# The last expert's down weights in column quarters, the second half as two transfers of 512 KB

## The reference

```python
def expert_block(args):
    e, xb = args
    gate, up = jnp.split(xb @ w_gate_up[e], 2, axis=-1)
    return (jax.nn.silu(gate) * up) @ w_down[e]
...
y = y_buf[dest] * gate_sorted[:, None].astype(xt.dtype)
out = jnp.zeros((N, D), xt.dtype).at[tok_sorted].add(y)
...
return rms_norm(h, norm_final)
```

## Time and profile before

| what | value |
|---|---|
| median of 3 runs | 660.54 us (660.26 to 660.78) |
| profiled execution | 661.26 us |
| its span, first to last instruction | 659.4 us |
| mean granted TensorE clock | 0.922 |
| TensorE busy | 514.9 us, 78% |
| VectorE, ScalarE busy | 228.5 us, 181.2 us |
| DMA | 238.12 MB, mean 361 GB/s |
| experts' weights in the chain that ended last | 43% |

### The profile page before, as it was taken

How to read it: one execution, slowest core, us unless ns; L and a number is a source line. 1 busy time by engine, 2 the same in 40 slices (tenths; PEclk the granted TensorE clock), 3 DMA queues, 4 the chain that set the end, 5 groups by cost and what they waited for, 6 DMA issues and landing times.

```text
span 659.4 us, 13368 instructions
## 1 busy us (share of the span) xinstructions
PE 514.9 (78%) x5842; PEld 376.5 (57%) x5842; DVE 228.5 (35%) x474; ACT 181.2 (27%) x400; POOL 27.2 (4%) x50
## 2 busy tenths in 40 slices
PE   8999999999999977886665854866585486658663
PEld 7988998789888755554333522533263253325431
DVE  4696896764653532221211311121121112112113
ACT  7659557264442021110111110010111001011113
POOL 1220202200000000000000000000000000000000
PEclk9999999999999998999878977887897788789888
DMA  8944744496579999999999999999999999999992
GB/s 332 372 157 170 313 166 151 135 415 218 192 295 371 373 393 428 425 438 435 436 433 427 427 429 432 432 435 429 435 429 438 438 435 435 429 409 426 426 396 82
DMA packets 16005, 238.12 MB, mean 361 GB/s; under 512 B 1760, under 2 KB 2016, under 8 KB 3424
## 3 DMA queue, kind: packets, MB, share of 16 engines
q1 hardware_dynamic: 15680, 236.94, 86.4%
q10 hardware_dynamic: 288, 0.63, 0.3%
HBM read 236.51 MB, written 1.05 MB: 360 GB/s over the span
## 4 chain that ended last, share of the span: by engine, by line
PE 47%; DMA 44%; DVE 2%; ACT 2%; issue 1%; SPq 1%; another core or an unknown queue 1%; POOL 1%; ACTq 0%; DVEq 0%; POOLq 0%
DMA ring<-in_w_expert 43%; PE psum L626 15%; PE psum L934 9%; PE psum L609 9%; PE psum L965 4%; PE psum L656 2%; PE psum L802 1%; PE psum L779 1%; PE psum L594 1%; SPq L457 1%; DMA res<-in_x 1%; PE psum L865 1%; PE psum L958 1%; POOL stat L1378 1%
## 5 line engine op out<-in xcount | busy, mean ns | idle before, releaser
L934 PE MATMUL psum<-ring,xg 128*32 128x256 f32 x2048 | 157.5, 469 | 85.1 <-DMA ring<-in_w_expert 78.0
L934 PEld LDWEIGHTS psum<-ring,xg 128*32 128x32 f32 x2048 | 75.8, 133 | 155.4 <-DMA ring<-in_w_expert 84.3
L626 PE MATMUL psum<-split_w,split_act 128*128 128x512 f32 x432 | 102.3, 393 | 0.9 <-DVE res L1642 0.9
L626 PEld LDWEIGHTS psum<-split_w,split_act 128*128 128x128 f32 x432 | 80.2, 188 | 17.8 <-DVE res L1642 1.3
L1314 ACT ACTIVATE small<-psum 128x128 f32<-128x128 f32 x32 | 8.9, 277 | 280.5 <-PE psum L934 280.5
L1855 DVE SCALAR_TENSOR_TENSOR small<-small,psum 128x128 f32<-128x128 f32 x32 | 9.2, 288 | 204.7 <-ACT small L1314 204.7
L1467 DVE TENSOR_TENSOR split_w<-landing,split_w 128x2048 fp32r<-128x2048 f32 x29 | 66.2, 2290 | 33.8 <-ACT split_w L1105 33.7
L1105 ACT ACTIVATE split_w<-landing 128x2048 fp32r<-128x2048 f32 (+1 forms) x31 | 57.5, 1863 | 46.5 <-PE psum L609 22.8
L1866 DVE COPY ybuf<-psum 32x128 f32<-32x128 f32 x128 | 37.2, 291 | 77.0 <-PE psum L965 76.2
L609 PE MATMUL psum<-split_act,split_w 128*128 128x256 f32 x480 | 58.2, 283 | 0.0
L609 PEld LDWEIGHTS psum<-split_act,split_w 128*128 128x128 f32 x480 | 57.8, 192 | 0.4 <-issue 0.3
(11 more groups left out here) (191 smaller groups left out, 407.7 us busy)
## 6 DMA issues: line engine op xcount, KB each, us to landing
ring<-in_w_expert SPq DMA_DIRECT2D x20, 6144.0 KB, 47.8
ring<-in_w_expert SPq DMA_DIRECT2D x23, 2048.0 KB, 31.6
landing<-in_dense SPq DMA_DIRECT2D x29, 1024.0 KB, 5.5
ring<-in_w_expert SPq DMA_DIRECT2D x26, 1024.0 KB, 8.3
res<-in_x SPq DMA_DIRECT2D x2, 512.0 KB, 4.2
landing<-in_dense SPq DMA_DIRECT2D x2, 512.0 KB, 7.2
work<-in_mem SPq DMA_DIRECT2D x1, 1024.0 KB, 13.8
ybuf<-in_late SPq DMA_DIRECT2D x1, 512.0 KB, 17.6
```

What stands on the lines that cost most here:

```text
L626: i = mm(b, tokens_of(src[t], k0 + k, h), w[a][:, k, :], start=first and k == 0 and n == 0, stop=last and k == CT - 1 and n == 2)
L934: i = mm(half[SLOTS * strip:SLOTS * strip + SLOTS], xg[:, CT * part + k, SLOTS * j:SLOTS * j + SLOTS], w[:, k, :, P * strip:P * strip + P] ...
```

## The change

`lay_out_experts` orders the down weights by column quarters: the 16 KB of a partition hold four blocks of 4 KB, one for each 256 output columns, and in a block the four chunks of the contraction. `expert_down` and `ov_down_w` follow; strip s of a side is in quarter s // 2 of that side. Whole-expert and whole-unit transfers are as they were.

The second half of the last down unit comes in two transfers of 512 KB, each with its own semaphore (`loaded[u][1]` and the new `last_quarter`). On TensorE, both scatters of columns 0 stand ahead of the products of that half. Each quarter is multiplied by `last_down(q)`, two strips for each chunk, quarter 0 into bank 4 and quarter 1 into bank 6; ScalarE and VectorE copy one strip each; `last_scatter(q)` adds 256 columns to both token halves.

```diff
 def lay_out_experts(inputs):
-    down = ....reshape(EXPERTS, CT, P, 2, 512).transpose(0, 2, 3, 1, 4)
+    down = ....reshape(EXPERTS, CT, P, 2, 2, 256).transpose(0, 2, 3, 4, 1, 5)
...
 def refill_down(g, j, by_sides):
                 sp.wait_ge(y_done, 2 * BATCH * g + (2 * (j - BATCH) + 2))
                 if by_sides:
-                    load_expert(BATCH * g + j, j, 2)
+                    u, w = EXPERT_UNITS[j][2], w_expert[BATCH * g + j][:, 2 * UNIT:]
+                    load_expert(BATCH * g + j, j, 2, (0,))
+                    sp.dma_start(unit(u)[:, HALF:HALF + D], w[:, HALF:HALF + D]).then_inc(loaded[u][1], 16)
+                    sp.dma_start(unit(u)[:, HALF + D:], w[:, HALF + D:]).then_inc(last_quarter, 16)
...
+            def last_down(q):
+                w = expert_down(BATCH - 1)
+                for k in range(CT):
+                    for strip in (2 * q, 2 * q + 1):
+                        i = mm(bank((GATHER, HY)[q])[SLOTS * strip:SLOTS * strip + SLOTS, 0:P],
+                               hidTs[(BATCH - 1) % 2][:, SLOTS * k:SLOTS * k + SLOTS],
+                               w[:, 1, q, k, P * (strip % 2):P * (strip % 2) + P],
+                               start=k == 0, stop=k == CT - 1, tile_position=(0, SLOTS * strip))
+                i.then_inc(quarter_done, 1)
+
+            def last_scatter(q):
+                pe.wait_ge(quarter_act, q + 1)
+                pe.wait_ge(quarter_dve, q + 1)
+                for h in range(NH):
+                    i = mm(bank(ACC_BANKS[2 * h + 1])[:, 256 * q:256 * q + 256], give[:, P * h:P * h + P],
+                           ybuf[:, 512 + 256 * q:768 + 256 * q], start=False, stop=True, skip_group_check=True)
+                    if q:
+                        i.then_inc(scattered, 1)
...
             down(g, 3, 0)
-            scatter(g, 0, (0,))
+            scatter(g, 0, range(NH))
             pe.wait_ge(loaded[u][1], 48)
-            down(g, 3, 1)
-            scatter(g, 0, (1,))
-            scatter(g, 1, range(NH))
+            await_y(2 * (EXPERTS - 1))
+            last_down(0)
+            last_scatter(0)
+            pe.wait_ge(last_quarter, 16)
+            last_down(1)
+            last_scatter(1)
...
-            for j in (2, 3):
-                gather_y(BATCHES - 1, j)
+            gather_y(BATCHES - 1, 2)
+            gather_y(BATCHES - 1, 3, (0,))
+            for q in range(2):
+                act.wait_ge(quarter_done, q + 1)
+                r, at = slice(2 * SLOTS * q, 2 * SLOTS * q + SLOTS), 512 + 256 * q
+                copy(ybuf[3 * SLOTS:, at:at + P], bank((GATHER, HY)[q])[r, 0:P]).then_inc(quarter_act, 1)
```

More of the change, by code:

```diff
@@ L144, in lay_out_experts @@
     gate_up = np.asarray(inputs["w_gate_up"])[0].reshape(EXPERTS, 2, CT, P, 2 * FF).transpose(0, 3, 1, 2, 4)
-    down = np.asarray(inputs["w_down"])[0].reshape(EXPERTS, CT, P, 2, 512).transpose(0, 2, 3, 1, 4)
+    down = np.asarray(inputs["w_down"])[0].reshape(EXPERTS, CT, P, 2, 2, 256).transpose(0, 2, 3, 4, 1, 5)
     return np.concatenate([gate_up.reshape(EXPERTS, P, 2 * UNIT), down.reshape(EXPERTS, P, UNIT)], axis=2)
@@ L391, in block_kernel @@
         scattered = sem("scattered")
+        last_quarter, quarter_done = sem("last_quarter"), sem("quarter_done")
+        quarter_act, quarter_dve = sem("quarter_act"), sem("quarter_dve")
         ov_normed, ov_turned, ov_xT = sem("ov_normed"), sem("ov_turned"), sem("ov_xT")
@@ L409, in block_kernel @@
         ov_gu_w = [unit(u).rearrange("p (c n) -> p c n", c=CT) for u in (0, 1)]
-        ov_down_w = unit(2).rearrange("p (s c n) -> p s c n", s=2, c=CT)
+        ov_down_w = unit(2).rearrange("p (s q c n) -> p s c q n", s=2, q=2, c=CT)
         ov_x = tiles(spare(9, 0, 2048), KC)
@@ L425, in expert_down @@
         def expert_down(j):
-            return unit(EXPERT_UNITS[j][2]).rearrange("p (s c n) -> p s c n", s=2, c=CT)
+            return unit(EXPERT_UNITS[j][2]).rearrange("p (s q c n) -> p s q c n", s=2, q=2, c=CT)
         def await_fill(eng, job):
@@ L965, in down @@
                         i = mm(bank((HY, GATHER)[side])[SLOTS * strip:SLOTS * strip + SLOTS, 0:P],
-                               hidTs[j % 2][:, SLOTS * k:SLOTS * k + SLOTS], w[:, side, k, P * strip:P * strip + P],
+                               hidTs[j % 2][:, SLOTS * k:SLOTS * k + SLOTS], w[:, side, strip // 2, k, P * (strip % 2):P * (strip % 2) + P],
                                start=k == 0, stop=k == CT - 1, tile_position=(0, SLOTS * strip))
                 i.then_inc(y_done, 1)
+            def last_down(q):
[15 more added lines that the diff above has]
+                        i.then_inc(scattered, 1)
             def down_whole(g, j, passes):
@@ L1320, in hidden, with gather_y @@
                 copy(hidTs[j % 2], bank(HY)[:, 256:256 + P]).then_inc(hidT_ready, 1)
-            def gather_y(g, j):
-                for side in range(2):
+            def gather_y(g, j, sides=range(2)):
+                for side in sides:
                     act.wait_ge(y_done, 2 * BATCH * g + (2 * j + side + 1))
@@ L1884, in _ @@
                 hidden(BATCHES - 1, j)
-            for j in (2, 3):
-                gather_y(BATCHES - 1, j)
+            gather_y(BATCHES - 1, 2)
+            gather_y(BATCHES - 1, 3, (0,))
+            for q in range(2):
+                dve.wait_ge(quarter_done, q + 1)
+                r, at = slice(2 * SLOTS * q + SLOTS, 2 * SLOTS * q + 2 * SLOTS), 512 + 256 * q + P
+                V.tensor_copy(ybuf[3 * SLOTS:, at:at + P], bank((4, 6)[q])[r, 0:P]).then_inc(quarter_dve, 1)
             many = dve.value_load(flag[0:1, 0:1])
```

## The result

In the times, the changed kernel takes 663.1 us (median of 6 runs, 662.45 to 664.44) where the kernel before takes 660.43 beside it. The ratio is 1.0043 with a 95% interval of 1.0029 to 1.0056, that is 1.9 to 3.7 us more. The prediction said 662.7 us, slower by 2.2.

What follows compares the result with a forecast made beforehand. The last weight transfer's landing at 647.13 sets the end; the change puts 3.4 us of work (0.85 + 1.08 + 0.50 + 0.94) where TensorE had 1.17 to spare: +2.2 on the median 660.54, so 662.7 us, range 661.2 to 664.4.

Steps and rivals of the forecast that it cites:

- Steps 1 and 2: Layout, whole-expert loads and earlier down products, and one more DMA issue on SP: each costs nothing.
- Step 3: Two 512 KB transfers in place of one of 1 MB: the last quarter lands 0.1 us later, about 647.25.
- Step 4: Both scatters of column half 0 ahead of the products fill TensorE's gap, cost nothing; next can start at 646.85.
- Step 5: First quarter's products on TensorE: two strips take 1.08 us, as a half does, ending at 647.93.
- Step 6: Ahead of the last products: wait for copies 0.50 us, then the first quarter's scatter 0.94, so 649.4.
- Step 7: Last quarter's products start at 649.4, landing covered by 2.1 us, and end at 650.45 against 648.25 before.
- Step 8: After the last products: one copy fewer gains nothing; squares still start 0.76 us later, 651.2 against 649.01.
- Rival D: Two-strip products on TensorE cost half of a half, 0.41 us less twice: +1.4, 661.9 us; chance 0.10.
- A: The sum holds, TensorE's own order decides the tail: 662.7 us, own range 662.1 to 663.3; chance 0.60.
- C: The last landing decides both kernels if halves land 6.2 us or more apart: not slower, 660.6 us; chance 0.10.
- E: TensorE's clock falls to half in the tail, from 645.05 on: +6.6, 667 us; chance 0.04.
- B: In timed runs the code load does not delay the kernel before's last half: +3.4, 663.9 us; chance 0.13.

Runs made afterwards that it cites:

- layout: The kernel before with only the new order of the down weights in DRAM and in the ring: 661.26 us, ratio 1.0000.
- split: The kernel before with the new layout and the second half in two 512 KB transfers, both awaited ahead of the old products: 660.91 us, ratio 0.9993.
- after: The changed kernel itself, against the kernel before: 663.1 us, ratio 1.0043.
- after_extra: The changed kernel with an unused extra 512 KB transfer between the two quarters: 662.89 us, ratio 1.0042 to the kernel before.
- order0: The kernel before, old layout and transfers, with only both scatters of columns 0 ahead of the wait for the second half: 661.74 us, ratio 1.0003.
- late_scatter: The changed kernel with the first quarter's scatter behind the second quarter's products: 661.48 us, ratio 1.0005 to the kernel before.
- before_extra: The kernel before with an unused extra 512 KB transfer between the two halves of the last down weights: 662.29 us, ratio 1.0028.
- before_pad: The kernel before with 48 products of 32 x 32 in TensorE's waits of the last group, to shift the code's blocks: 661.4 us, ratio 1.0008.
- after_again: The changed kernel measured once more, against the kernel before: 663.46 us, ratio 1.0037.
- quarter_first: The changed kernel with the first quarter multiplied right behind half 0, ahead of both scatters of columns 0: 660.87 us, ratio 1.0001 to the kernel before.

## Why the prediction was right

1. Steps 1 and 2, layout and one more issue, cost nothing that can be measured: `layout` at 1.0000; SP's third issue took 4.2 us from 607.92, 40 us ahead of its landing.
2. Step 3, the landing 0.1 us later: `split` shows no loss. In the changed kernel the last quarter landed 3.6 us after half 0's products started, where half 1 did after 4.0 before. It was not the bound in either kernel of this order (`after`, `after_extra`). The step puts 1.5 us of the gap of 4.01 down to the code load; its packet holds an engine for 1.1 us, and no row shows the other 0.4.
3. Step 4: the first quarter's products start 1.88 us after the first scatter, forecast 1.80. In the trace of `order0` this move alone is free.
4. Step 5: 16 records of two strips take 1.07 us, forecast 1.08. Rival D, 0.67, is out. The prediction cites the Trainium skill for this step ("TensorE: Matmul & The Clock Gate", section "Why this matters for your kernels"): small outputs gain from column tiles that run at once. The trace agrees: 16 records of two tiles take 1.07 us, 32 of four take 1.08.
5. Step 6: from the products' end (649.91) to the scatter 0.48, forecast 0.50. The four records of 256 columns hold TensorE until 651.42, 1.03 us, forecast 0.94. Half the price of 512 columns was right (eight such records take 1.97 us in `late_scatter`, four 1.10, so 0.22 each). What the first record costs on top was taken 0.08 too small here and in step 4; no run shows what it consists of.
6. Step 7: the last products start 6.36 us after half 0's, forecast 6.24, with the landing covered by 2.8 us, forecast 2.1. `after_extra` shows the cover: 1.5 us of it can be used up without any change of time that can be measured.
7. Step 8: the squares start 0.73 us after the products' end, forecast 0.76, although a copy of 0.27 us has gone. ScalarE now idles ahead of the square, with no engine named, where the flag load runs.

The sum was +2.2 and the trace has +2.3. The ratios say 2.8 (1.9 to 3.7) and, again, 2.4 (1.6 to 3.3). The likeliest case, A, is the one that came. That the sum fits the one pair of profiles to 0.1 us is in part luck, since the gap between the halves' products in the old order is not the same in every execution. `layout` has 3.89:

```profile
643.13 1.08 PE L965 MATMUL psum<-ring,more_hidT 128*32 128x128 f32 x32
...
647.02 1.08 PE L965 MATMUL psum<-ring,more_hidT 128*32 128x128 f32 x32 [0.92 <-DMA ring<-in_w_expert]
```

`split` has 3.49. Against the 6.36 of the changed kernel these gaps give losses of 2.5 and 2.9 us, an estimate, where 4.01 gives 2.35. The ratios lie in this range. Of the rivals, C (the landing decides both) is excluded by `after_extra`, and D by the trace. E did not come in the changed kernel: from half 0's products on, the clock stood at 1.00 in both of its profiles. That it can come in this tail is seen in `before_extra`. The row of 632 to 634 that E goes by has TensorE busy for all of its 2 us, at 0.50.

B asked whether the timed runs of the kernel before have the code load in the way. Its +3.4 lies within the first interval (to 3.7) and just above the second (to 3.3), so the times do not exclude it. Against it stand the profiles of `layout`, `split` and `order0`: in each a packet of 16 KB on the instruction queue holds an engine for 1.1 us, beginning between 644.0 and 645.5, about where half 0's products end, as in the kernel before. The measured size does not need B. It stays open as a part of the spread: an execution whose gap is 2.91, as in `before_pad`, would lose 3.45.

The prediction took the profiled execution's 0.72 us above the median for a constant of profiling. It is rather the spread from run to run: the profiled execution lies 1.5 us below the median in `late_scatter` and 1.7 above it in `after_again`. Whether the clock in stretches that wait for weights makes this spread was not measured. None of this changed the forecast.

What the change was meant to do, it did: a quarter lands and is multiplied earlier. But the wait for half 1 had left TensorE only 1.0 us idle in the row of 647.17 (1.17 as the prediction counts), and the new order put 3.5 us of work into that place, of which 1.5 (waiting for copies, scattering the first quarter) had been free behind the last products.

## What to carry to other kernels

When the last transfer is cut into pieces, look at what the engine does between the pieces. Here each piece brought a wait for copies and a scatter ahead of the last piece's products, and an engine that runs in order took them at full price; issued behind the last products (`late_scatter`), or with the copies' wait filled by the next piece (`quarter_first`), the same work cost nothing that could be measured. Count the idle time that the late landing really leaves (1.0 to 1.2 us here) before filling it, and price a piece by its serial steps: half of the strips is not half of the time. Products in different strips of the array are best issued without a wait between them: two quarters took 1.54 us together and 1.07 each, and a half with its four strips in turn 1.08.

## What was not expected of the hardware

- Two groups of products in different column strips overlapped in part when nothing stood between them: 32 records in 1.54 us (`late_scatter`), 16 in 1.07.
- A wait of TensorE for weights was followed by a fall of the clock in one execution and not in another. In `before_extra`, after a wait of 1.12 us, the granted clock stood at 0.65 for 648 to 650 and at 0.50 for 650 to 652, and products of 1.08 us took 1.81. In the kernel before, after the same kind of wait, 1.02 us, it stood at 1.00 up to 654. That the wait is the cause is not shown.
- An extra DRAM-to-DRAM transfer of 512 KB in the same queue moved the last landing of the changed kernel from 3.56 to 5.02 us after half 0's products, some 1.5 us in this pair of executions. Its packets of 4 KB, eight for each engine, would take 1.3 us by the earlier trace rows, an estimate.
